# Chunks 3 to 7: VectorE adds up 768 of the 1024 columns of a V row and TensorE 256, instead of 512 each

## The chip, the core and the metric

The kernel runs on one core of one Trainium2 chip, in one launch, with all inputs in HBM. The metric is the device time of that launch in microseconds (us).

## What is computed

One decoder layer over 1024 tokens of width 1024, in float32: two groups of attention heads side by side (eight MLA heads and eight dilated-window heads), an attention over 256 memory tokens, and then PEER, a layer of single-neuron experts. The part that matters here is PEER. For each token 8 heads pick 16 experts each out of 16384, so 128 picks a token; each pick has a row of `u_tab` (dotted with the token) and a row of `v_tab` (added to the token's result with the resulting coefficient), each of 1024 float32 numbers:

```python
def peer_ffn(xn, w_q, sub_keys, u_tab, v_tab):
    def chunk(xc):                                   # 128 tokens
        ...                                          # top 16 x 16 keys -> expert (c, 8, 16), best_s
        g = jax.nn.softmax(best_s, axis=-1)
        u = u_tab[expert]
        a = jax.nn.gelu(jnp.einsum('cd,chkd->chk', xc, u), approximate=False)
        coeff = g * a
        return jnp.einsum('chk,chkd->cd', coeff, v_tab[expert])

h = h + mixed @ w_out                                # both attention groups
h = h + memory_attention(...)
h = h + peer_ffn(rms_norm(h, norm_ffn), ...)
out = rms_norm(h, norm_final)
```

## The kernel before

Tokens are worked on in 8 chunks of 128, one token a partition. After the weights have been folded (`fold_weights`) and the projections made (`project_tokens`), the attention of chunks 0 to 2 runs alone. From then on the expert rows flow in all the time. `Stream` holds their order: `ROWS` lists 2048 rows, ("u", g) or ("v", g) for pick g, U rows 22 picks ahead of V rows at first. One row is one indirect DMA that GpSimd issues (`Stream.gpsimd`, L264): for each of the 128 tokens it fetches the 4 KB of that token's expert, 512 KB in all, into one of the 8 slots of `s_ring`. A slot is free for a new row when its old row has been used: a U row by VectorE, a V row by all engines that add it up (L248 to L254).

- A U row is multiplied with the token and summed on VectorE (L380, `s_dots`). ScalarE makes Gelu of 16 dots at a time (L282), VectorE the coefficient (L368).
- A V row is multiplied with its coefficient and added to the result. TensorE does it as a matmul with a diagonal matrix of the coefficients (L454, into PSUM: `a_acc` here, `e_acc` elsewhere); the diagonal is made by ScalarE (L310, `s_diagonal`), three of them in turn. VectorE does it as a `scalar_tensor_tensor` on `s_h` in SBUF (L387).

`STAGES` says who does what. In rows 0 to 214 (picking of chunks 0 to 2) and from row 640 on (picking of chunks 3 to 7) the mode is "pe": TensorE adds up all 1024 columns. In rows 215 to 639 the mode is "split": TensorE takes columns 0 to 511 and VectorE columns 512 to 1023. These 425 rows, 212 U and 213 V, run beside the attention of chunks 3 to 7 (`attend`, first = 3), which needs six of the eight PSUM banks for itself. In this stage the token vector that U rows are multiplied with stands in SBUF (`s_x`); in the other two it is copied to PSUM (`x_copy`).

`attend` goes through 80 units, one head of one chunk each. In a unit of nb key blocks TensorE transposes the probabilities (L1297, nb of them), makes the scores of the unit after the next (L1242 or L1246) and multiplies probabilities with values (L1257); VectorE adds the bias table and takes the maximum (L1158), ScalarE does the exponential (L1108) and the copy of the transposed block (L1129). After each unit every engine works off its share of the rows, up to `rows_until[n]`, which grows with nb + 3 and in one unit of each chunk by 44 more, where the output projection of the chunk before (L1275, 32 matmuls of 512 columns) runs with rows between the matmuls. Every engine runs its instructions in the order written; no scheduler reorders them. At the end of a chunk of picks (two ends fall into the stage) VectorE adds TensorE's sum to `s_h` (L426), and at the end of the stage `flush` does (L416). A barrier ends the stage; then the last stage begins.

Of the kernel before, what the change touches and what calls it, by code (L numbers as in the profile page):

```python
# [9 lines left out]
ALU = mybir.AluOpType  # L10
# [100 lines left out]
class Stream:  # L111
# [5 lines left out]

    def __init__(self, nc, io, sb, sb_early, sem, stages):  # L120
        self.nc, self.io = nc, io
        self.stages = [(start, until, mode) for start, (until, mode) in zip([0] + [u for u, _ in stages], stages)]
        self.ident = sb("s_ident", [P, P])
        self.eps = sb("s_eps", [P, 1])
        self.h = sb("s_h", [P, D])
# [9 lines left out]
        self.more_slots = None  # L135
        self.acc = None
        self.x_copy = None

        self.row_loaded = [sem(f"s_row_loaded{i}") for i in range(WIDE_RING)]
        self.x_kept = [sem(f"s_x_kept{c}") for c in range(CHUNKS)]  # L140
# [25 lines left out]
        for n in range(len(ROWS)):  # L166
            s = next(i for i, (start, until, _) in enumerate(self.stages) if start <= n < until)
            kind = ROWS[n][0]
            pe += kind == "v"
            dve += kind == "v" and self.stages[s][2] == "split"  # L170
            self.stage_of.append(s)
            self.pe_through.append(pe)
            self.dve_through.append(dve)
            if n == wide_from:
                free = list(range(RING, WIDE_RING)) + free
            slot = free.pop(0)
            free.append(slot)
            self.slot.append(slot)
            self.before.append(last_in.get(slot))
            last_in[slot] = n  # L180
# [28 lines left out]
        return self.stages[self.stage_of[n]][2]  # L209

    def pe_columns(self, n):
        return D if self.mode(n) == "pe" else BANK

    def row(self, n):
        slot = self.slot[n]
# [24 lines left out]
    def gpsimd(self, until):  # L240
        pool = self.nc.gpsimd
        for n in range(self.at["gpsimd"], min(until, len(ROWS))):
            kind, g = ROWS[n]
            c, k = divmod(g, PICKS)
            paired = n >= PAIRS_AT
            if paired and kind == "v":
                continue
            for m in {self.before[n], self.before[n + 1] if paired else None} - {None}:  # L248
                if ROWS[m][0] == "u":
                    pool.wait_ge(self.u_used, ROWS[m][1] + 1)  # L250
                else:
                    pool.wait_ge(self.v_pe, self.pe_through[m])
                    if self.mode(m) == "split":
                        pool.wait_ge(self.v_dve, self.dve_through[m])  # L254
            if kind == "u" and k % (2 * TOPK) == 0:
                pool.wait_ge(self.expert_ready, GROUPS * c + k // (2 * TOPK) + 1)
            pool.sem_inc(self.passed_pool, 1)
            slot = self.slot[n]
            table = self.io["peer_uv" if paired else "peer_u" if kind == "u" else "peer_v"]
            to = self.row(n)  # L260
            if paired:
                to = self.ring[:, slot:slot + 2, :] if slot < RING else self.more_slots[:, slot - RING:slot - RING + 2, :]
                to = to.rearrange("p s d -> p (s d)")
            pool.indirect_dma_start(out=to, out_offset=None, in_=table,  # L264
                                    in_offset=bass.IndirectOffsetOnAxis(ap=self.expert[c % PICK_BUFFERS][:, k:k + 1], axis=0)
                                    ).then_inc(self.row_loaded[self.slot[n]], 16)
        self.at["gpsimd"] = max(until, self.at["gpsimd"])
# [63 lines left out]

    def end_root(self, c):
        act = self.nc.scalar
        act.wait_ge(self.h3_ready, c + 1)
        need(act, self.out_stored, 16 * c)
        if c + 1 < CHUNKS and LAST_U[c] >= self.stages[-1][0]:
            act.wait_ge(self.x_copied, self.copies[len(self.stages) - 1, c + 1])
        act.activation(self.scratch[:, :], self.h[:, :], ACT.Square, accum_out=self.end_stat[:, 0:1]).then_inc(self.end_squared, 1)
        act.wait_ge(self.end_squared, c + 1)
        act.activation(self.end_stat[:, 1:2], self.end_stat[:, 0:1], ACT.Sqrt, scale=1.0 / D,  # L340
                       bias=self.eps[:, :]).then_inc(self.end_rooted, 1)
        act.dma_start(self.scratch[:, :], self.io["norm_final_row"].partition_broadcast(P)).then_inc(self.final_loaded, 16)
# [9 lines left out]
    def vector(self, until):  # L352
        dve = self.nc.vector
        for n in range(self.at["vector"], until):
            kind, g = ROWS[n]
            c, k = divmod(g, PICKS)
            if n in self.end_sum_at:
                self.end_sum(self.end_sum_at[n], self.stage_of[n])
            if n in self.end_out_at:
                self.end_out(self.end_out_at[n])  # L360
            if n in COEFF_AT:
                i = COEFF_AT[n]
                d, h = divmod(i, PEER_HEADS)
                at = slice(TOPK * h, TOPK * (h + 1))
                gate = self.gate[d % PICK_BUFFERS][:, h, :]
                dve.wait_ge(self.gate_ready, GROUPS * d + h // 2 + 1)
                dve.wait_ge(self.activated, i + 1)
                dve.tensor_tensor(gate, self.active[:, at], gate, ALU.mult).then_inc(self.coeff_ready, 1)  # L368
            row = self.row(n)
            if kind == "u":  # L370
                s = self.stage_of[n]
                copied = self.mode(n) == "pe"
                if k == 0 or n in self.first_u:
                    if copied:
                        dve.wait_ge(self.x_copied, self.copies[s, c])
                    else:
                        dve.wait_ge(self.x_loaded, 16 * self.x_loads[s, c])
                self.wait_row(dve, n)
                x = self.x_copy if copied else self.x
                dve.tensor_tensor_reduce(row, row, x[:, :], 1.0, 0.0, ALU.mult, ALU.add,  # L380
                                         self.dots[:, k:k + 1]).then_inc(self.u_used, 1)
            elif self.mode(n) == "split":
                self.wait_row(dve, n)
                dve.wait_ge(self.coeff_ready, g // TOPK + 1)
                self.wait_h(c, self.dve_through[n] - 1)
                half = slice(BANK, D)
                dve.scalar_tensor_tensor(self.h[:, half], row[:, half], self.coeff(g), self.h[:, half], ALU.mult,  # L387
                                         ALU.add).then_inc(self.v_dve, 1)
        self.at["vector"] = max(until, self.at["vector"])

    def picks_free(self, c):

# [26 lines left out]
    def end_sum(self, c, s):  # L419
        dve = self.nc.vector  # L420
        last = CHUNK_END[c]
        dve.wait_ge(self.v_pe, self.pe_through[last])
        self.wait_h(c, self.dve_through[last])
        group = self.group(c, s)
        columns = slice(0, self.pe_columns(group[-1]))
        dve.tensor_tensor(self.h[:, columns], self.acc[:, columns], self.h[:, columns], ALU.add).then_inc(self.h3_ready, 1)  # L426
        dve.wait_ge(self.h3_ready, c + 1)

    def end_out(self, c):
        dve = self.nc.vector  # L430
# [7 lines left out]
    def tensor(self, until):  # L438
        pe = self.nc.tensor
        for n in range(self.at["tensor"], until):  # L440
            kind, g = ROWS[n]
            if kind == "u":
                continue
            c = g // PICKS
            s = self.stage_of[n]
            group = self.group(c, s)
            if n == group[0] and c > 0 and self.group(c - 1, s):
                pe.wait_ge(self.h3_ready, c)
            made = self.pe_through[n]
            pe.wait_ge(self.diagonal_ready, made)  # L450
            self.wait_row(pe, n)
            row = self.row(n)
            for at in range(0, self.pe_columns(n), BANK):
                last = pe.matmul(self.acc[:, at:at + BANK], self.diagonal[:, made % DIAGONALS, :], row[:, at:at + BANK],  # L454
                                 start=(n == group[0]), stop=(n == group[-1]))
            last.then_inc(self.v_pe, 1)
        self.at["tensor"] = max(until, self.at["tensor"])
# [902 lines left out]
def pick_chunks(nc, io, stream, chunks, events, until, resident):  # L1360
# [6 lines left out]
    with ExitStack() as ctx:  # L1367
# [16 lines left out]
        b.gain = stream.scratch if gain_kept else b.h  # L1384
        stream.acc = ps("e_acc", [P, D])
        stream.x_copy = ps("e_x_copy", [P, D])
        block = ctx.enter_context(nc.Block())

        def table_of(f, number):
# [376 lines left out]


PICK_02, ATTEND_37 = 215, 640
STAGES = [(PICK_02, "pe"), (ATTEND_37, "split"), (len(ROWS), "pe")]


def hybrid_layer(nc, io):
# [80 lines left out]
```

## Time and profile before

| | us |
|---|---|
| three runs | 4079.92, 4094.79, 4095.18 |
| their median | 4094.79 |
| the profiled execution, its own time | 4086.41 |
| its span, first to last instruction | 4084.6 |
| the stage with the attention of chunks 3 to 7, in that span | 1322 to 2048 |

Busy time over the whole span: TensorE (PE) 3284.0 us (80%), VectorE (DVE) 2166.0 us (53%), GpSimd (POOL) 1374.5 us (34%), ScalarE (ACT) 1300.4 us (32%). These are averages over stages with different limits, so for this change only the rows of the stage count. Busy matmuls are pipelined, and a busy PE is not a PE at its peak. In a row of a timeline the first number is the start, the second the duration; in brackets stands the idle time of the engine just before and who ended it. "issue" is a gap in which the engine waited for nothing that the profile shows.

### The profile page before, as it was taken

To read this page: it belongs to the slowest core of one execution; us is meant where nothing else is said; L and a number is where in the kernel's file an instruction comes from. 1 tells how busy PE (TensorE), PEld (TensorE's weight loads), DVE (VectorE), ACT (ScalarE), POOL (GpSimd) and SP (SyncE) were. 2 spreads that over 40 slices of the span, in tenths; PEclk is the share of its full clock that TensorE was granted. 3 is DMA by queue.
4 is the path that set the end of the run, shared out by engine and by line. 5 is a ranking of instruction groups with operands and counts; after the bars stand their busy time and mean duration, and the time that the engine had idled before them with its cause. 6 is when DMAs were issued, how large, how long until landed. Compare 5 with 4: busy or idle time off the path is not lost. (4 is left out here: it accounts for less than half of the span.)

```text
span 4084.6 us, 33485 instructions
## 1 busy us (share of the span) xinstructions
PE 3284.0 (80%) x9134; PEld 1561.4 (38%) x9134; DVE 2166.0 (53%) x4954; ACT 1300.4 (32%) x3397; POOL 1374.5 (34%) x1367
## 2 busy tenths in 40 slices
PE   8689888758784878887869689779878977987776
PEld 6544445323232444544433234234323423432222
DVE  0311112166847667766615745854774585477444
ACT  1011113211221434433323433443443344344333
POOL 0000000024533767766612233333333332333332
PEclk9889997879897899999989899999999999999999
DMA  7610112499997999998978799999999999999998
GB/s 290 226 55 23 32 51 103 141 330 384 333 326 265 363 343 368 355 376 306 361 315 300 294 372 394 420 370 379 415 383 368 405 417 359 376 416 412 422 420 354
DMA packets 283743, 1288.75 MB, mean 316 GB/s; under 512 B 27440, under 2 KB 52144, under 8 KB 193072
## 3 DMA queue, kind: packets, MB, share of 16 engines
q0 software_dynamic: 195120, 1073.83, 67.5%
q1 hardware_dynamic: 83696, 195.62, 13.1%
q10 hardware_dynamic: 4752, 17.30, 1.2%
q8 instruction: 69, 1.13, 0.1%
q14 instruction: 106, 0.87, 0.1%
HBM read 1243.65 MB, written 42.99 MB: 315 GB/s over the span
## 5 line engine op out<-in xcount | busy, mean ns | idle before, releaser
L454 PE MATMUL e_acc<-s_ring,s_diagonal 128*128 128x512 f32 x2296 | 1149.1, 629 | 353.0 <-ACT s_diagonal L310 307.4
L380 DVE CUSTOM_DVE_ANT_0 s_ring<-s_ring,e_x_copy 128x1024 f32<-128x1024 f32 x581 | 704.9, 1217 | 460.3 <-DMA s_ring<-peer_uv,s_expert 399.5
L454 PEld LDWEIGHTS e_acc<-s_ring,s_diagonal 128*128 128x128 f32 x2296 | 427.8, 197 | 1026.9 <-ACT s_diagonal L310 549.4
L264 POOL DMA_INDIRECT s_ring<-peer_uv,s_expert x462 | 435.9, 943 | 868.0 <-PE e_acc L454 687.4
L454 PE MATMUL e_acc<-e_more_slots,s_diagonal 128*128 128x512 f32 x948 | 469.8, 622 | 108.1 <-ACT s_diagonal L310 98.7
L310 ACT ACTIVATE s_diagonal<-s_ident,s_gate 128x128 f32<-128x128 f32 x1024 | 396.8, 398 | 333.3 <-PE e_acc L454 221.1
L264 POOL DMA_INDIRECT s_ring<-peer_u,s_expert x331 | 358.1, 1082 | 398.8 <-DVE s_expert L1637 232.7
L264 POOL DMA_INDIRECT s_ring<-peer_v,s_expert x325 | 347.5, 1069 | 346.9 <-PE e_acc L454 123.3
L327 ACT ACTIVATE s_dots<-s_dots 128x1 f32<-128x1 f32 x704 | 141.5, 201 | 943.2 <-DVE s_dots L380 941.9
L380 DVE CUSTOM_DVE_ANT_0 e_more_slots<-e_more_slots,e_x_copy 128x1024 f32<-128x1024 f32 x231 | 281.0, 1218 | 209.7 <-DMA e_more_slots<-peer_uv,s_expert 207.3
L264 POOL DMA_INDIRECT e_more_slots<-peer_uv,s_expert x231 | 218.4, 945 | 435.5 <-PE e_acc L454 329.1
L454 PE MATMUL a_acc<-s_ring,s_diagonal 128*128 128x512 f32 x426 | 242.9, 675 | 106.7 <-DMA s_ring<-peer_v,s_expert 53.9
L454 PEld LDWEIGHTS e_acc<-e_more_slots,s_diagonal 128*128 128x128 f32 x948 | 174.1, 195 | 382.7 <-ACT s_diagonal L310 205.8
L380 DVE CUSTOM_DVE_ANT_0 s_ring<-s_ring,s_x 128x1024 f32<-128x1024 f32 x212 | 259.5, 1224 | 111.3 <-DMA s_ring<-peer_u,s_expert 100.2
L1225 POOL TENSOR_SCALAR a_w_out<-a_w_out,a_gain_mix 128x1024 f32<-128x1024 f32 x8 | 8.8, 1109 | 616.8 <-DMA a_w_out<-w_out 616.8
L329 ACT ACTIVATE s_gate<-s_dots,s_gate 128x1 f32<-128x1 f32 x704 | 207.3, 294 | 22.9
L1129 ACT ACTIVATE a_probs_t<-a_turned 128x128 f32<-128x128 f32 (+7 forms) x128 | 83.3, 651 | 375.7 <-PE a_turned L1297 371.1
L1696 PE MATMUL e_product<-e_halves,e_rows_t 128*128 128x512 f32 x384 | 180.1, 615 | 11.7 <-ACT e_rows_t L1472 7.8
L387 DVE SCALAR_TENSOR_TENSOR s_h<-s_ring,s_gate,s_h 128x512 f32<-128x512 f32 x213 | 160.2, 752 | 48.0 <-DMA s_ring<-peer_v,s_expert 35.1
L1257 PE MATMUL a_heads_out<-values,a_probs_t 128*128 128x64 f32 x1152 | 165.4, 292 | 17.1 <-ACT a_probs_t L1129 15.0
L1257 PEld LDWEIGHTS a_heads_out<-values,a_probs_t 128*128 128x128 f32 x1152 | 152.4, 205 | 69.4 <-ACT a_probs_t L1129 50.1
L1696 PE MATMUL e_product<-e_peer_scores,e_rows_t 128*128 128x512 f32 x320 | 159.1, 592 | 0.0
(206 smaller groups left out, 3423.9 us busy)
## 6 DMA issues: line engine op xcount, KB each, us to landing
e_halves<-peer_scores SPq DMA_DIRECT2D x12, 2048.0 KB, 16.1
e_halves<-mem_scores SPq DMA_DIRECT2D x6, 2048.0 KB, 14.7
e_halves<-mem_values SPq DMA_DIRECT2D x6, 2048.0 KB, 19.7
p_w_in<-w_in SPq DMA_DIRECT2D x8, 1104.0 KB, 15.4
f_w_big<-w_mem_kv SPq DMA_DIRECT2D x4, 2048.0 KB, 15.7
f_w_big<-peer_w_q_t SPq DMA_DIRECT2D x2, 4096.0 KB, 17.8
peer_scores<-f_stage_s SPq DMA_DIRECT2D x16, 512.0 KB, 3.6
s_ring<-peer_uv,s_expert POOLq DMA_INDIRECT x462, 8.8
```

The lines of the kernel that those rows point to most:

```text
L264: pool.indirect_dma_start(out=to, out_offset=None, in_=table, in_offset=bass.IndirectOffsetOnAxis(ap=self.expert[c % PICK_BUFFERS][:, k:k ...
L310: act.activation(self.diagonal[:, made % DIAGONALS, :], self.ident[:, :], ACT.Copy, scale=self.coeff(g)).then_inc(self.diagonal_ready, 1)
L327: act.activation(self.active[:, k:k + 1], self.dots[:, k:k + 1], ACT.Gelu).then_inc(self.activated_alone, 1)
L329: act.activation(self.coeff(g), self.active[:, k:k + 1], ACT.Copy, scale=self.coeff(g)).then_inc(self.coeff_made, 1)
L380: dve.tensor_tensor_reduce(row, row, x[:, :], 1.0, 0.0, ALU.mult, ALU.add, self.dots[:, k:k + 1]).then_inc(self.u_used, 1)
L387: dve.scalar_tensor_tensor(self.h[:, half], row[:, half], self.coeff(g), self.h[:, half], ALU.mult, ALU.add).then_inc(self.v_dve, 1)
L454: last = pe.matmul(self.acc[:, at:at + BANK], self.diagonal[:, made % DIAGONALS, :], row[:, at:at + BANK], start=(n == group[0]), stop=(n ...
L1129: act.activation(probs_t[:, u % 2, 0:P * nb], turned[:, 0:P * nb], ACT.Copy).then_inc(p_t_ready, 1)
L1225: pool.tensor_scalar(w_out[:, k, :], w_out[:, k, :], gain_mix[:, k:k + 1], 1.0, ALU.mult, ALU.mult).then_inc(w_gained, 1)
L1257: last = pe.matmul(heads_out[:, HEAD * h:HEAD * (h + 1)], probs_t[:, u % 2, P * k:P * (k + 1)], keep["values"][:, k, HEAD * u:HEAD * (u + ...
L1696: made = pe.matmul(bank, b.rows_t[:, P * k:P * (k + 1)], table_of(f, number)[:, k, :], start=(k == 0), stop=(k == DT - 1))
```

## The change

`STAGES` gets a third number for each stage, the columns that TensorE takes of a V row: 1024, 256 and 1024. `pe_columns` reads it. In rows 215 to 639 the matmuls of L454 are then 128x256 instead of 128x512, the additions of L387 128x768 instead of 128x512, and the three additions of TensorE's sum to `s_h` (L426 twice, L416 once) 128x256 instead of 128x512. The number and the order of the instructions on every engine stay as they are, the waits too. The new function `add_part`, which lets VectorE take columns in a "pe" stage as well, is not called with these numbers, and `summed(c)` is c + 1.

```diff
-        self.stages = [(start, until, mode) for start, (until, mode) in zip([0] + [u for u, _ in stages], stages)]
+        self.stages = [(start, until, mode) for start, (until, mode, _) in zip([0] + [u for u, _, _ in stages], stages)]
+        self.columns = [columns for _, _, columns in stages]
...
     def pe_columns(self, n):
-        return D if self.mode(n) == "pe" else BANK
+        return self.columns[self.stage_of[n]]
+
+    def summed(self, c):
+
+        return sum(1 + (self.mode(CHUNK_END[d]) == "pe" and self.pe_columns(CHUNK_END[d]) < D) for d in range(c + 1))
...
-                half = slice(BANK, D)
-                dve.scalar_tensor_tensor(self.h[:, half], row[:, half], self.coeff(g), self.h[:, half], ALU.mult,
+                rest = slice(self.pe_columns(n), D)
+                dve.scalar_tensor_tensor(self.h[:, rest], row[:, rest], self.coeff(g), self.h[:, rest], ALU.mult,
                                          ALU.add).then_inc(self.v_dve, 1)
+            elif self.pe_columns(n) < D:
+                if n < PAIRS_AT:
+                    self.add_part(n)
...
             for at in range(0, self.pe_columns(n), BANK):
-                last = pe.matmul(self.acc[:, at:at + BANK], self.diagonal[:, made % DIAGONALS, :], row[:, at:at + BANK],
+                to = min(at + BANK, self.pe_columns(n))
+                last = pe.matmul(self.acc[:, at:to], self.diagonal[:, made % DIAGONALS, :], row[:, at:to],
                                  start=(n == group[0]), stop=(n == group[-1]))
...
-STAGES = [(PICK_02, "pe"), (ATTEND_37, "split"), (len(ROWS), "pe")]
+STAGES = [(PICK_02, "pe", D), (ATTEND_37, "split", D // 4), (len(ROWS), "pe", D)]
```

## Rows read from the trace of the kernel before

**Rows 1.** Window of the stage: length, busy time (x instructions) of PE, PEld, DVE, ACT, POOL; clock, DMA share, GB/s

```profile
1560.00:1680.00 120.00, 103.89 (x396) 58.03 (x396) 86.51 (x144) 42.58 (x88) 84.83 (x77) 0.94 0.99 374
```

**Rows 2.** Groups by form, 1320 to 2030 us: busy, mean ns; idle before

```profile
L380 DVE CUSTOM_DVE_ANT_0 s_ring<-s_ring,s_x 128x1024 f32<-128x1024 f32 x212 | 259.5, 1224 | 111.3 <-DMA s_ring<-peer_u,s_expert 100.2 <-DMA s_x<-next_x 10.6
L454 PE MATMUL a_acc<-s_ring,s_diagonal 128*128 128x512 f32 x426 | 242.9, 675 | 106.7 <-DMA s_ring<-peer_v,s_expert 53.9 <-ACT s_diagonal L310 32.1 <-issue 20.0
L264 POOL DMA_INDIRECT s_ring<-peer_u,s_expert x208 | 240.0, 1154 | 77.3 <-issue 58.6 <-DVE s_dots L380 10.8 <-DVE s_h L387 4.2
L264 POOL DMA_INDIRECT s_ring<-peer_v,s_expert x214 | 239.0, 1117 | 165.9 <-issue 49.7 <-DVE s_dots L380 46.4 <-DVE s_h L387 42.1
L387 DVE SCALAR_TENSOR_TENSOR s_h<-s_ring,s_gate,s_h 128x512 f32<-128x512 f32 x213 | 160.2, 752 | 48.0 <-DMA s_ring<-peer_v,s_expert 35.1 <-DMA s_h<-next_h 10.0
```

**Rows 3.** What GpSimd waited for, 1330 to 2020 us: total, times, longest

```profile
POOL s_ring L264 <- issue: 106.1, 337, 1.2
POOL s_ring L264 <- DVE s_h L387: 46.3, 26, 14.1
POOL s_ring L264 <- DVE s_dots L380: 36.0, 18, 5.7
POOL s_ring L264 <- PE a_acc L454: 31.5, 33, 3.3
```

**Rows 4.** Line 264 over the whole span, and the page on DMA issues: us to landing

```profile
DMA to landing us min/median/max: 4.1/7.7/46.2
...
s_ring<-peer_u,s_expert POOLq DMA_INDIRECT x331, 6.5
```

**Rows 5.** Timeline: a V row's matmuls, then the projection's

```profile
1583.65 1.02 PE L454 MATMUL a_acc<-s_ring,s_diagonal 128*128 128x512 f32 x2
1584.51 1.02 PE L1275 MATMUL a_turned<-a_w_out,a_mixed_t 128*128 128x512 f32 x2
```

**Rows 6.** Groups by form: one VectorE operation at two widths, a matmul at 256

```profile
L1158 DVE CUSTOM_DVE_ANT_0 a_probs<-a_scores,a_tables 128x768 f32<-128x768 f32 x16 | 15.2, 952 | 0.7 <-PE a_scores L1242 0.7
...
L1158 DVE CUSTOM_DVE_ANT_0 a_probs<-a_scores,a_tables 128x512 f32<-128x512 f32 x16 | 11.0, 686 | 8.4 <-PE a_scores L1242 8.4
...
L1242 PE MATMUL a_scores<-mla_k_t,a_q_mla 96*128 96x256 f32 x16 | 4.8, 379 | 0.0
```

**Rows 7.** GpSimd's groups in the stage before, 1100 to 1200 us

```profile
L264 POOL DMA_INDIRECT s_ring<-peer_u,s_expert x22 | 21.1, 960 | 6.7 <-issue 6.7
L264 POOL DMA_INDIRECT s_ring<-peer_v,s_expert x22 | 20.8, 943 | 52.1 <-PE e_acc L454 36.9 <-DVE s_dots L380 14.5 <-issue 0.6
```

**Rows 8.** Timeline: long issues on GpSimd, and VectorE beside them

```profile
1331.17 0.74 DVE L387 SCALAR_TENSOR_TENSOR s_h<-s_ring,s_gate,s_h 128x512 f32<-128x512 f32 x1
1331.44 1.29 POOL L264 DMA_INDIRECT s_ring<-peer_v,s_expert  x1 [0.30 <-issue]
...
1339.25 1.87 POOL L264 DMA_INDIRECT s_ring<-peer_u,s_expert  x1 [0.30 <-issue]
1340.34 0.75 DVE L387 SCALAR_TENSOR_TENSOR s_h<-s_ring,s_gate,s_h 128x512 f32<-128x512 f32 x1
...
2028.57 1.50 POOL L264 DMA_INDIRECT s_ring<-peer_v,s_expert  x1 [0.30 <-issue]
2029.19 0.75 DVE L387 SCALAR_TENSOR_TENSOR s_h<-s_ring,s_gate,s_h 128x512 f32<-128x512 f32 x1
```

**Rows 9.** What VectorE waited for on TensorE, 1320 to 2050 us

```profile
DVE a_mixed_t L1182 <- PE a_turned L1265: 21.5, 5, 6.7
DVE a_probs L1158 <- PE a_scores L1242: 12.3, 8, 5.5
```

**Rows 10.** Timeline: scores matmuls before and after a long wait of TensorE

```profile
1653.80 1.55 PE L1246 MATMUL a_scores<-dil_k_t,a_q_dil 64*128 64x512 f32 x4
...
1661.64 1.10 PE L454 MATMUL a_acc<-s_ring,s_diagonal 128*128 128x512 f32 x2 [2.41 <-DMA s_ring<-peer_v,s_expert]
...
1663.57 2.93 PE L1246 MATMUL a_scores<-dil_k_t,a_q_dil 64*128 64x512 f32 x4
```

More of the change, by code:

```diff
@@ L121, in __init__ @@
         self.nc, self.io = nc, io
-        self.stages = [(start, until, mode) for start, (until, mode) in zip([0] + [u for u, _ in stages], stages)]
+        self.stages = [(start, until, mode) for start, (until, mode, _) in zip([0] + [u for u, _, _ in stages], stages)]
+        self.columns = [columns for _, _, columns in stages]
+        assert all(mode == "split" or columns == D or s == len(stages) - 1 for s, (_, mode, columns) in enumerate(stages))
         self.ident = sb("s_ident", [P, P])
@@ L137, in __init__ @@
         self.x_copy = None
+        self.part = None
         self.row_loaded = [sem(f"s_row_loaded{i}") for i in range(WIDE_RING)]
@@ L169, in __init__ @@
             pe += kind == "v"
-            dve += kind == "v" and self.stages[s][2] == "split"
+            dve += kind == "v" and self.columns[s] < D
             self.stage_of.append(s)
@@ L252, in gpsimd @@
                     pool.wait_ge(self.v_pe, self.pe_through[m])
-                    if self.mode(m) == "split":
+                    if self.pe_columns(m) < D:
                         pool.wait_ge(self.v_dve, self.dve_through[m])
@@ L333, in end_root @@
         act = self.nc.scalar
-        act.wait_ge(self.h3_ready, c + 1)
+        act.wait_ge(self.h3_ready, self.summed(c))
         need(act, self.out_stored, 16 * c)
@@ L385, in vector, with add_part @@
                 self.wait_h(c, self.dve_through[n] - 1)
-                half = slice(BANK, D)
-                dve.scalar_tensor_tensor(self.h[:, half], row[:, half], self.coeff(g), self.h[:, half], ALU.mult,
+                rest = slice(self.pe_columns(n), D)
+                dve.scalar_tensor_tensor(self.h[:, rest], row[:, rest], self.coeff(g), self.h[:, rest], ALU.mult,
                                          ALU.add).then_inc(self.v_dve, 1)
-        self.at["vector"] = max(until, self.at["vector"])
+            elif self.pe_columns(n) < D:
+                if n < PAIRS_AT:
+                    self.add_part(n)
+                elif n - 2 >= PAIRS_AT:
+                    self.add_part(n - 2)
+                if n == len(ROWS) - 1:
+                    self.add_part(n)
+        self.at["vector"] = max(until, self.at["vector"])
+    def add_part(self, n):
+        dve = self.nc.vector
+        g = ROWS[n][1]
+        rest = slice(self.pe_columns(n), D)
+        row, part = self.row(n)[:, rest], self.part[:, :]
+        self.wait_row(dve, n)
+        if g >= ALONE_FROM:
+            dve.wait_ge(self.coeff_made, g - ALONE_FROM + 1)
+        else:
+            dve.wait_ge(self.coeff_ready, g // TOPK + 1)
+        if n == self.group(g // PICKS, self.stage_of[n])[0]:
+            dve.tensor_scalar(part, row, self.coeff(g), None, ALU.mult).then_inc(self.v_dve, 1)
+        else:
+            dve.wait_ge(self.v_dve, self.dve_through[n] - 1)
+            dve.scalar_tensor_tensor(part, row, self.coeff(g), part, ALU.mult, ALU.add).then_inc(self.v_dve, 1)
     def picks_free(self, c):
@@ L426, in end_sum @@
         dve.tensor_tensor(self.h[:, columns], self.acc[:, columns], self.h[:, columns], ALU.add).then_inc(self.h3_ready, 1)
-        dve.wait_ge(self.h3_ready, c + 1)
+        if self.mode(last) == "pe" and columns.stop < D:
+            rest = slice(columns.stop, D)
+            dve.tensor_tensor(self.h[:, rest], self.part[:, :], self.h[:, rest], ALU.add).then_inc(self.h3_ready, 1)
+        dve.wait_ge(self.h3_ready, self.summed(c))
     def end_out(self, c):
@@ L447, in tensor @@
             if n == group[0] and c > 0 and self.group(c - 1, s):
-                pe.wait_ge(self.h3_ready, c)
+                pe.wait_ge(self.h3_ready, self.summed(c - 1))
             made = self.pe_through[n]
@@ L1386, in pick_chunks @@
         stream.x_copy = ps("e_x_copy", [P, D])
+        if resident and stream.columns[-1] < D:
+            stream.part = sb("e_part", [P, D - stream.columns[-1]])
         block = ctx.enter_context(nc.Block())
```

## The prediction

> **What bounds the kernel now.** I looked for the stage that the change touches and asked in it which wait ends last. The stage runs from 1322 to 2048 us, 726 of the 4084.6 us, and ends in a barrier; nothing outside it changes.
>
> One window first [rows 1]. TensorE is busy 87% of it, VectorE 72%, and the 16 DMA engines 99%. GpSimd shows 84.83 us, which looks like 71%, but the gap of 0.30 us behind each issue isn't counted as busy [rows 8]: 77 x (1.10 + 0.30) = 108 of 120 us. So rows of experts come in about as fast as GpSimd can issue them and the DMA engines can carry them. TensorE's high share says nothing yet.
>
> Then the groups [rows 2]. VectorE and TensorE both wait for rows: VectorE 100.2 us for U rows and 35.1 for V rows, TensorE 53.9 for V rows. An engine that waits so much for its input isn't what sets the pace; it is fed.
>
> Last, what GpSimd waits for [rows 3]. The four lines and the busy time make up the 690 us: 470 busy in 414 issues, 106.1 of plain gaps (337 times, 0.31 each), 82.3 waiting for VectorE to free a slot (44 times, one end of a chunk with 14.1 among them) and 31.5 waiting for TensorE (33 times). In 337 of 414 cases nothing held GpSimd but its own instructions. **The stage is bound by GpSimd's issuing, with the DMA engines right behind**, and slots that are freed late cost 114 us at most. Of these TensorE has the smaller part.
>
> A cushion comes with it. A row lands 6.5 us (median) after its issue, against 4.1 at the least [rows 4]. Some 2.4 us of that is a queue in front of busy DMA engines, so an issue that comes a little later or earlier shows up only in part in when its row lands. I take one half for this below, an estimate from the DMA share of 0.99 (no idle time to recover) and the queue (which can run dry in waits over 2.4 us).
>
> **What the change takes from TensorE.** A V row costs it 0.86 us, from the start of its two matmuls to the start of the next ones [rows 5]. Half the columns should be half of that, 0.43 us; a matmul of 256 columns is there (379 ns against 675 for 512, with latency in both [rows 2, 6]), so the saving is not under 0.30 x 2 either. I take 0.43: 213 x 0.43 = 92 us of TensorE's time. It isn't on the path that sets the end except where somebody waits for TensorE. Those places are:
> - GpSimd's 33 waits for TensorE, 31.5 us [rows 3]. The gap of 0.30 stays in each, so 21.6 us can go. But a V slot is freed by both engines, and VectorE now leaves it later: it is late next. I take half, 11.
> - VectorE's 13 waits for the turned block and for scores [rows 9]. Each can shrink by what TensorE gains in a unit of two V rows, 0.86: 11 us, and half of it, 6, as the others are short.
>
> The bound is 33 us of gain; I take 17, and half of it behind the DMA queue: **-8 us**.
>
> **What it adds on VectorE.** VectorE's time grows with the width by 952 - 686 = 266 ns for 256 columns [rows 6]. L387 goes from 752 [rows 2] to 1018 ns: 213 x 0.266 = 57 us, or 8% of the stage on top of 72%. Behind L387 on VectorE stands the next U row or the next maximum (L1158), and behind these ScalarE's exponential and TensorE's transposes. Of the 135 us that VectorE waits for rows, 57 can be filled, so most of it is hidden. Where it has a backlog it isn't: GpSimd waited 44 times for a slot of VectorE, and each wait grows by 0.27 us for every V row in the backlog; one gives 12, two give 24, none gives 0. One V row lies between two frees, so I take 12, and half of it: **+6 us**.
>
> **What it does to GpSimd.** Nothing in GpSimd's code changes, and yet its instructions would. In the stage before this one an issue takes 0.95 us [rows 7], here 1.14 [rows 2]: over 422 issues 77 us more. The difference between the stages is that L380 reads both inputs from SBUF here (`s_x`), as L387 does. The timeline shows where the time goes [rows 8]. The issue at 1339.25 ends at 1341.12, and L387 beside it at 1341.09; the one at 2028.57 ends at 2030.07, L387 at 2029.94. I went through all 427 issues of the stage: 182 take over 0.98 us. Of these 72 end within 0.15 us behind an L387 (the two are the first and the last), 38 end 0.8 us behind the end of an L387 that ran when they began (the first is the one at 1331.44, ending at 1332.73, L387 at 1331.91), and 63 the same way behind an L380. So GpSimd is held until VectorE's instruction is over. L387 becomes 0.266 us longer, and the 110 issues that it holds are held so much longer: 110 x 0.266 = 29 us. If the stretch grows only with VectorE's time in such instructions, it is 57 / 420 x 77 = 10 us. Between the two I take 20, nearer to the count, since I saw the ends coincide, but less, since some issues will fall elsewhere. GpSimd sets the pace, so half of it gets through: **+10 us**.
>
> The Trainium skill, SBUF — State Buffer, "Who interferes with whom", says that a VectorE instruction with two SBUF inputs contends with a GpSimd one that reads SBUF, but infers that descriptor generation isn't held by it, because it needs the write side. The trace contradicts that inference [rows 7, 8]. By the inference this term would be 0 and the sum 10 us lower, still no change.
>
> **The rest.** The three additions of TensorE's sum lose 0.27 us each, and TensorE's last two V rows before the final projection 0.4 us each: **-1 us**. ScalarE's work stays as it is.
>
> **Sum.** -8 + 6 + 10 - 1 = +7 us. The profiled execution took 4086.4 us, 1.8 more than its span, and would take 4093. It lies 8 us under the median of the three runs and 4 under their mean, 4090.0, which I build on because the three spread over 15 us: **4097 us**.
>
> **Rivals.**
> - *TensorE is the bound after all.* For: it is busy 87%, more than any other compute engine. If all that was waited for it comes back and VectorE's longer additions vanish in its waits for rows: -33 us, 4057 us, faster. Against: TensorE itself waits 53.9 us for rows, and the DMA engines have hardly a gap. Chance 0.17.
> - *VectorE holds GpSimd.* Slower by one mechanism: every one of the 110 held issues is held 0.266 us longer, and the DMA queue doesn't cushion it since the delay comes again and again: +29, with the 12 of late slots whole, less 8: +33 us, 4123 us. It decides as soon as more than about two thirds of the 29 us reach the stage's end. For: the ends that coincide [rows 8], and 337 issues with nothing else in front [rows 3]. Against: the queue of 2.4 us. Chance 0.31.
> - *TensorE's clock.* Less work on it means more pauses, and behind a pause of 2.41 us four matmuls took 2.93 us instead of 1.55 [rows 10], the lower of the two clocks, 1.2 instead of 2.4 GHz. If the granted clock fell from 0.94 to 0.85, 18% more of 726 us would run at half speed and cost TensorE about 65 us of work. That is less than the 92 it is given, so the time would be that of the forecast. I count it there.
>
> **How the numbers follow.** A measurement of this kernel can tell about 0.5% (20 us) from no change. Forecast (within 0.5%) 0.52, slower 0.31, faster 0.17. The bounds of the terms together reach from -34 (33 + 1, nothing lost) to +53 (29 + 24, nothing won), 4056 to 4143; cut to eight in ten this is 4062 to 4135. The likeliest case alone has 4070 to 4110.
>
> **What would show it.** In the profile after: L387 at about 1018 ns; L454 of `a_acc` with half the start-to-start time; GpSimd's mean issue in the stage up from 1.14 to about 1.18 us, with ends that still coincide with L387's (at 1.14 or less that term is wrong); GpSimd's waits for TensorE under 20 us and for VectorE over 82; VectorE's waits for rows down from 135 us; the barrier at 2048 moved by less than 20 us. If the barrier comes 30 us earlier and GpSimd's waits shrink on both engines, the pace was TensorE's, and my reading of rows 3 was wrong. If it comes 30 us later with issues at 1.2 us or more, the halving was wrong.

## The result and the profile after

The changed kernel takes 4101.09 us (median of 20 runs, 4089.95 to 4108.11), the kernel before 4087.07 us (20 runs, 4079.53 to 4096.43). The ratio is 1.0033, with a 95% interval of 1.0024 to 1.0042: 14 us slower, within the 0.5% that were called no change. Timed again beside other kernels (e10 below) it was 1.0038 (1.0024 to 1.0052).

The profiled execution of the changed kernel has a span of 4097.8 us. Its stage with the attention of chunks 3 to 7 ends with the barrier at 2064.7 us, where it ended at 2047.7 before. That is 17 us later, 1 of which was already there when the stage began. So the loss is in the stage. (A span is that of one execution; the runs of one kernel spread over 17 to 18 us here, so a few microseconds between two profiles mean nothing by themselves.) The stage of both kernels as one window each, before first (columns as in rows 1):

```profile
1322.00:2048.00 726.00, 601.44 (x2350) 338.68 (x2350) 506.51 (x860) 269.03 (x535) 481.84 (x425) 0.93 0.94 352
```
```profile
1323.00:2065.00 742.00, 577.11 (x2350) 388.25 (x2349) 559.42 (x860) 269.71 (x535) 509.30 (x425) 0.82 0.93 344
```

Three numbers moved. VectorE is 53 us busier, as it should be. GpSimd is 27.5 us busier, although nothing in its code was changed. And TensorE is only 24 us less busy, with its granted clock down from 0.93 to 0.82. The 27.5 us are of one profile each: in a second profile of the changed kernel (e10) GpSimd's 425 issues take 497.2 us, 15 us more than before, at the same loss of time. So GpSimd's growth lies between 15 and 28 us. These are the groups by form of the changed kernel that answer to [rows 2]:

```profile
L388 DVE CUSTOM_DVE_ANT_0 s_ring<-s_ring,s_x 128x1024 f32<-128x1024 f32 x212 | 259.2, 1223 | 77.3 <-DMA s_ring<-peer_u,s_expert 65.6 <-DMA s_x<-next_x 11.1
L490 PE MATMUL a_acc<-s_ring,s_diagonal 128*128 128x256 f32 x426 | 161.9, 490 | 143.3 <-DMA s_ring<-peer_v,s_expert 84.4 <-ACT s_diagonal L318 37.0 <-issue 21.5
L272 POOL DMA_INDIRECT s_ring<-peer_u,s_expert x208 | 245.3, 1179 | 76.4 <-issue 46.0 <-DVE s_h L395 12.9 <-DVE s_dots L388 10.7
L272 POOL DMA_INDIRECT s_ring<-peer_v,s_expert x214 | 261.2, 1221 | 153.3 <-PE a_acc L490 52.2 <-issue 47.9 <-DVE s_h L395 44.3
L395 DVE SCALAR_TENSOR_TENSOR s_h<-s_ring,s_gate,s_h 128x768 f32<-128x768 f32 x213 | 217.0, 1019 | 56.1 <-DMA s_ring<-peer_v,s_expert 44.0 <-DMA s_h<-next_h 9.9
```

L395 takes 1019 ns, as worked out. TensorE waits more for V rows (84.4 us instead of 53.9): it comes to them earlier, or they come later; the rows shown don't tell which. VectorE waits less for rows (110 us instead of 135): it has less time to spare. The matmuls of V rows lost 81 us of busy time, but TensorE as a whole only 24, so its other matmuls in the stage grew by 57 us. The largest of their groups, before first and then after (busy us, mean ns); the transposes of L1297 went from 293 to 332 ns:

```profile
L1257 PE MATMUL a_heads_out<-values,a_probs_t 128*128 128x64 f32 x960 | 125.9, 283 | 11.4 <-ACT a_probs_t L1129 9.9 <-DVE a_mixed L1169 1.5
```
```profile
L1293 PE MATMUL a_heads_out<-values,a_probs_t 128*128 128x64 f32 x960 | 143.1, 307 | 11.5 <-ACT a_probs_t L1165 9.9 <-DVE a_mixed L1205 1.6
```

What GpSimd waited for in the changed kernel, 1330 to 2035 us, against [rows 3]:

```profile
POOL s_ring L272 <- issue: 92.1, 302, 0.3
POOL s_ring L272 <- PE a_acc L490: 59.0, 49, 19.6
POOL s_ring L272 <- DVE s_h L395: 56.9, 56, 15.0
POOL s_ring L272 <- DVE s_dots L388: 19.5, 8, 4.7
```

The 19.6 us are the start of the stage, a wait that lay just outside the window before and was put down to VectorE there. Without it GpSimd waits 39.4 us for TensorE (31.5 before) and 76.4 for VectorE (82.3 before). The account of GpSimd's time is then +27.5 busy, -14 in plain gaps, +8 and -6: the stage's 16 us. The term that stands out is GpSimd's own busy time. Where it comes from shows in the timeline. This is one of 71 such pairs of the changed kernel:

```profile
1587.37 1.02 DVE L395 SCALAR_TENSOR_TENSOR s_h<-s_ring,s_gate,s_h 128x768 f32<-128x768 f32 x1
1587.65 1.54 POOL L272 DMA_INDIRECT s_ring<-peer_v,s_expert  x1 [0.30 <-issue]
```

The issue begins at 1587.65 while L395 runs, L395 ends at 1588.39, and the issue ends 0.80 us later, at 1589.19, where an undisturbed one takes 0.94 us in all. Below, an issue is called held when it takes over 0.98 us and ends 0.8 us behind a VectorE instruction that ran when it began; the hold is what it takes over 0.94 us.

### The profile page after: what moved, and what is told of

Read it like the earlier page. It is cut to its first block and busy times, and to the rows that moved or that the text cites. A ratio compares the mean times of both kernels' runs of the same rounds, so it can differ in the third digit from the quotient of the medians.

```text
span 4097.8 us, 33485 instructions
## 1 busy us (share of the span) xinstructions
PE 3257.8 (80%) x9134; PEld 1612.5 (39%) x9134; DVE 2219.0 (54%) x4954; ACT 1301.5 (32%) x3397; POOL 1403.2 (34%) x1367
## 3 DMA queue, kind: packets, MB, share of 16 engines
q8 instruction: 69, 1.13, 0.1%
## 5 line engine op out<-in xcount | busy, mean ns | idle before, releaser
L388 DVE CUSTOM_DVE_ANT_0 s_ring<-s_ring,e_x_copy 128x1024 f32<-128x1024 f32 x581 | 704.9, 1217 | 465.2 <-DMA s_ring<-peer_uv,s_expert 403.0
L272 POOL DMA_INDIRECT s_ring<-peer_v,s_expert x325 | 369.7, 1137 | 332.4 <-PE e_acc L490 123.2
L388 DVE CUSTOM_DVE_ANT_0 e_more_slots<-e_more_slots,e_x_copy 128x1024 f32<-128x1024 f32 x231 | 281.0, 1218 | 210.4 <-DMA e_more_slots<-peer_uv,s_expert 208.0
L388 DVE CUSTOM_DVE_ANT_0 s_ring<-s_ring,s_x 128x1024 f32<-128x1024 f32 x212 | 259.2, 1223 | 77.3 <-DMA s_ring<-peer_u,s_expert 65.6
L490 PE MATMUL a_acc<-s_ring,s_diagonal 128*128 128x256 f32 x426 | 161.9, 490 | 143.3 <-DMA s_ring<-peer_v,s_expert 84.4
L395 DVE SCALAR_TENSOR_TENSOR s_h<-s_ring,s_gate,s_h 128x768 f32<-128x768 f32 x213 | 217.0, 1019 | 56.1 <-DMA s_ring<-peer_v,s_expert 44.0
L1293 PEld LDWEIGHTS a_heads_out<-values,a_probs_t 128*128 128x128 f32 x1152 | 171.9, 227 | 73.3 <-ACT a_probs_t L1165 47.2
L1293 PE MATMUL a_heads_out<-values,a_probs_t 128*128 128x64 f32 x1152 | 184.4, 315 | 15.8 <-ACT a_probs_t L1165 13.7
L490 PEld LDWEIGHTS a_acc<-s_ring,s_diagonal 128*128 128x128 f32 x426 | 85.1, 231 | 208.5 <-issue 146.9
## 6 DMA issues: line engine op xcount, KB each, us to landing
e_halves<-mem_values SPq DMA_DIRECT2D x6, 2048.0 KB, 19.6
```

The source lines that it names most:

```text
L395: dve.scalar_tensor_tensor(self.h[:, rest], row[:, rest], self.coeff(g), self.h[:, rest], ALU.mult, ALU.add).then_inc(self.v_dve, 1)
L490: last = pe.matmul(self.acc[:, at:to], self.diagonal[:, made % DIAGONALS, :], row[:, at:to], start=(n == group[0]), stop=(n == group[-1]))
L1293: last = pe.matmul(heads_out[:, HEAD * h:HEAD * (h + 1)], probs_t[:, u % 2, P * k:P * (k + 1)], keep["values"][:, k, HEAD * u:HEAD * (u + ...
```

## Experiments

The two theories: **A**, the change costs time because VectorE's longer instruction with two SBUF inputs holds GpSimd's issues longer; in a second form, because VectorE's longer time makes everything behind it later, whoever is held. **B**, the loss is TensorE's, which is slower with the lower clock. The runs came in three sessions (e1 to e4; e7 to e10; e5, e6, e11 and e12), and their times for the kernel before differ (medians 4109, 4099 and 4090 us). So each ratio is against runs of the kernel before from the same session, and spans of different sessions aren't compared. The changed kernel was timed with the result and in the second session, not in the first and the third, so a comparison of e3, e4 or e12 with it is one of two ratios. 12 us are 0.3%.

### e1 and e2: each half of the change alone

```diff
-                half = slice(BANK, D)
+                half = slice(BANK // 2, D)
```

> VectorE's half of the change alone: L387 of the kernel before takes columns 256 to 1023 (768 wide), TensorE keeps its 512, so columns 256 to 511 are added twice. Theory A (GpSimd's issues are held by VectorE's longer two-input instructions, 479 us of issues becoming 506 in the changed kernel): GpSimd's issues take about 506 us here too, TensorE's clock in the stage stays near 0.93, and the time is that of the changed kernel or more, +14 to +20 us over the kernel before. Theory B (the loss is TensorE's, whose granted clock in the stage fell from 0.93 to 0.82 and which made all its other matmuls there 57 us longer): with TensorE's work back the clock is back, and the time is within 5 us of the kernel before.

Measured: 1.0024 (1.0004 to 1.0043), +10 us; window 1322 to 2066:

```profile
1322.00:2066.00 744.00, 597.27 (x2327) 335.39 (x2328) 560.00 (x862) 269.67 (x537) 495.69 (x423) 0.92 0.93 343
```

```diff
-        return D if self.mode(n) == "pe" else BANK
+        return D if self.mode(n) == "pe" else BANK // 2
```

> TensorE's half of the change alone: the matmuls of a V row in the split stage are 256 wide, VectorE keeps its 512, so columns 256 to 511 are not added at all. Theory A (VectorE holds GpSimd): issues stay near 479 us, and TensorE's relief is worth 0 to -8 us. Theory B (TensorE's clock): the clock in the stage falls to 0.85 or less though VectorE does nothing more, GpSimd waits for TensorE as long as before or longer, and the time is +5 to +15 us.

Measured: 1.0003 (0.9989 to 1.0016), no difference.

```profile
1322.00:2066.00 744.00, 570.24 (x2353) 383.89 (x2351) 507.94 (x864) 270.78 (x540) 474.93 (x429) 0.83 0.94 348
```

VectorE's half costs time with the clock at 0.92. TensorE's half costs nothing, though it alone brings the clock to 0.83. Theory B doesn't explain a loss of 14 us: e2's interval ends at +7. But e2 says something else too: TensorE's relief brought nothing. The V rows' matmuls lost 83 us of busy time (159.7 us left of 242.9), TensorE as a whole 31 (601 to 570), the rest went to slower matmuls elsewhere, and GpSimd waited longer for TensorE than before, not less. e1's GpSimd takes 1.17 us an issue (495.69 us for 423) against 1.13 before; that is what e10, the changed kernel again, shows too, though not the 506 us that were expected. The interval allows anything from +2 to +18 us; its lower end is just clear of none.

### e3 and e4: the same time on VectorE with one SBUF input

```diff
-                dve.scalar_tensor_tensor(self.h[:, rest], row[:, rest], self.coeff(g), self.h[:, rest], ALU.mult,
-                                         ALU.add).then_inc(self.v_dve, 1)
+                dve.tensor_reduce(self.h[:, D - 1:D], row[:, D - 836:D], AX_X, ALU.max).then_inc(self.v_dve, 1)
```

> The changed kernel with L395 replaced by a reduction of 836 columns of the row, of about the same duration (1.02 us) but with one SBUF input instead of two; V rows are thus not added up on VectorE. Theory A: what held GpSimd behind a V row's addition is gone, its issues in the stage fall from 506 us by the 30 us that stand behind L395 to about 476, and the time falls by 10 to 20 us, to about the kernel before or under it. Theory B: nothing changes for TensorE, so the time stays within 5 us of the changed kernel.

Measured: 1.0007 (0.9988 to 1.0026). The reduction takes as long as the addition did, 1021 ns against 1019, and all waits are still there:

```profile
L395 DVE TENSOR_REDUCE s_h<-s_ring 128x1 f32<-128x836 f32 x213 | 217.5, 1021 | 53.3 <-DMA s_ring<-peer_v,s_expert 37.2 <-DMA s_h<-next_h 9.5 <-issue 4.1
...
L272 POOL DMA_INDIRECT s_ring<-peer_v,s_expert x217 | 243.9, 1124 | 193.3 <-PE a_acc L489 83.6 <-issue 50.9 <-DVE s_h L395 46.8
L272 POOL DMA_INDIRECT s_ring<-peer_u,s_expert x208 | 231.5, 1113 | 83.7 <-issue 49.3 <-DVE s_h L395 16.4 <-DVE s_dots L388 13.4
```

GpSimd is busy for 475 us (243.9 + 231.5), 34 less than in the changed kernel, and of the 14 us 3 are left (the interval reaches from -5 to +11). VectorE's time and TensorE's work are the same as in the changed kernel, and the clock is even lower (0.80), so neither can be what the loss came from. Against e10's profile GpSimd is busy 22 us less, not 34.

The edit takes away two things, the second input and the 768 columns of output (the reduction writes one). Which of them holds GpSimd, the trace of the kernel before tells. Outside the stage L380 writes the same 1024 columns to SBUF and takes as long, but its second input stands in PSUM:

```profile
L380 DVE CUSTOM_DVE_ANT_0 s_ring<-s_ring,e_x_copy 128x1024 f32<-128x1024 f32 x581 | 704.9, 1217 | 460.3 <-DMA s_ring<-peer_uv,s_expert 399.5 <-DMA s_ring<-peer_u,s_expert 60.6
```

410 issues of GpSimd begin while it runs so, and none takes over 0.945 us. Inside the stage, with `s_x` in SBUF, 142 of 158 are held. So it is the second input from SBUF, not the output.

e4 does the same to U rows as well (`dve.tensor_reduce(self.dots[:, k:k + 1], row, AX_X, ALU.add)` in place of L388).

> As the run before, and the products of U rows in the split stage (L388) also replaced by a reduction of all 1024 columns (same 1.22 us, one SBUF input), so the dots are wrong. Theory A: no issue of GpSimd is held any more, 0.94 to 0.96 us each, about 400 us in the stage instead of 506; if GpSimd's issuing sets the pace, the time falls by 40 to 70 us under the changed kernel; if the DMA engines stand right behind it, only by 15 to 30. Theory B: within 5 us of the changed kernel.

Measured: 0.9995 (0.9978 to 1.0011). Now nothing holds GpSimd, and each issue takes 0.937 us:

```profile
L272 POOL DMA_INDIRECT s_ring<-peer_v,s_expert x217 | 203.2, 936 | 267.0 <-PE a_acc L492 118.8 <-DVE s_h L398 56.4 <-issue 44.7
L272 POOL DMA_INDIRECT s_ring<-peer_u,s_expert x208 | 194.8, 937 | 78.9 <-issue 61.0 <-DVE s_h L398 7.7 <-DVE s_dots L392 6.8
```

398 us instead of 509, but the time is only that of the kernel before, some 16 to 18 us under the changed one. That is the branch of theory A in which something else stands right behind GpSimd's issuing. What GpSimd saved it spends waiting for slots, most of it for TensorE (118.8 us in front of V rows). With e3 it says that the hold costs time only in part of its range.

### e10, e7, e8 and e9: what the kernel before is bound by

> The changed kernel itself, beside the three runs below on the same chip. It was 14 us over the kernel before; VectorE's half alone was 10 us over it and TensorE's half alone within 2. Both theories expect +10 to +16 us.

Measured: 1.0038 (1.0024 to 1.0052).

e7 is the kernel before with the edits of e4, 580 columns for a V row (754 ns, where the addition took 752).

> The kernel before, with both of VectorE's instructions on rows of the split stage replaced by reductions of about the same duration with one SBUF input (1024 columns for a U row, 580 for a V row, 0.75 us); dots and the V half on VectorE are thus wrong. The same at VectorE's 768 columns and TensorE's 256 was at the time of the kernel before. Theory A1 (the change costs time only by holding GpSimd): without the holding the widths don't matter, and this is also at the kernel before, within 5 us. Theory A2 (the longer time on VectorE itself costs, since slots come free later and the next maximum starts later; the holding costs besides): this is 10 to 20 us under the kernel before.

Measured: 0.9998 (0.9985 to 1.0011). GpSimd is busy for 398 us as in e4. With nobody holding GpSimd, VectorE's width (e4 against e7) makes no difference: -0.05% and -0.02% against the kernel before. This is theory A in its first form. In its second form VectorE's longer time would cost by itself, and e7 would lie 10 to 20 us lower. (The two were timed in different sessions, and each interval is some 6 us wide on either side.)

e8 is e7 with half the bytes:

```diff
+            if self.mode(n) == "split":
+                to, table = to[:, 0:BANK], table.rearrange("n (two d) -> (n two) d", two=2)
```

> As the run before, and in the split stage each indirect DMA fetches 2 KB for a token instead of 4 (from the table seen as 32768 rows of 512), so that half of each slot keeps old numbers; GpSimd's issues, TensorE and VectorE do the same work. If the DMA engines bound the stage: its DMA share falls from 0.93 to about 0.5 and the time by 60 us or more. If GpSimd's issuing or the waits among the compute engines bound it: the time falls by less than 25 us.

Measured: 0.9967 (0.9948 to 0.9986), -13 us.

```profile
1322.00:2066.00 744.00, 608.13 (x2349) 350.88 (x2348) 494.12 (x648) 270.64 (x541) 406.84 (x429) 0.89 0.68 209
```

Halving the bytes of the rows and freeing GpSimd at once gives 13 us of a stage of 726. The DMA share falls only to 0.68, not to 0.5. So neither the DMA engines nor GpSimd set the pace alone; some 13 us under them (6 to 21) something else does. Which chain that is wasn't tested; the attention's own over TensorE, ScalarE and VectorE is the likely one, and TensorE is busy 82% of the window.

> The kernel before with L387 on 256 columns instead of 512 (columns 512 to 767 are not added at all), 0.49 us instead of 0.75; TensorE as before. The widening from 512 to 768 cost 10 us. Theory A (VectorE's time counts): the same step the other way, -5 to -12 us. If VectorE's width counts only above a threshold: within 3 us of the kernel before.

Measured: 1.0009 (0.9992 to 1.0025), no difference, and no gain of 5 to 12 us: a miss for theory A as it was put there. GpSimd is busy for 466 us. Neither here nor in e7 does less holding than in the kernel before (482 us) bring anything.

### e12 and e11: whose second input it is, and with TensorE's clock kept

e12 is the changed kernel with only the U rows' products as a reduction.

> The changed kernel, with the U rows' products of the split stage (L388) replaced by a reduction with one SBUF input (same 1.22 us; the dots are wrong), and the V rows' additions left as they are, 768 columns with two SBUF inputs. In the traces so far most of what GpSimd is held stands behind U rows (141 issues against 66). Theory A1 (the total that GpSimd is held decides, whichever instruction does it): its issues fall from about 500 us to 430 or less, and the time to within 5 us of the kernel before. Theory C (something about the V rows' additions themselves costs, such as their own two reads): the time stays at +10 to +16 us.

Measured: 0.9970 (0.9953 to 0.9988), 12 us under the kernel before, some 27 under the changed one.

```profile
L272 POOL DMA_INDIRECT s_ring<-peer_v,s_expert x217 | 223.4, 1030 | 193.5 <-PE a_acc L493 56.5 <-DVE s_h L398 49.3 <-issue 45.5
L272 POOL DMA_INDIRECT s_ring<-peer_u,s_expert x208 | 219.8, 1056 | 82.2 <-issue 49.9 <-DVE s_dots L392 15.1 <-PE a_acc L493 9.0
...
L398 DVE SCALAR_TENSOR_TENSOR s_h<-s_ring,s_gate,s_h 128x768 f32<-128x768 f32 x213 | 216.4, 1016 | 50.5 <-DMA s_ring<-peer_v,s_expert 37.4 <-DMA s_h<-next_h 10.0
```

The wide addition with two inputs is still there (1016 ns), and the loss is gone all the same, as GpSimd's total fell (443 us). That speaks against the addition itself as the cause. But the run is better than theory A expected, and better than e4, e7 and e9, which say that less holding than before brings nothing. That isn't explained. e4 and e12 were timed in different sessions, and their intervals (0.9978 to 1.0011, 0.9953 to 0.9988) overlap a little.

> TensorE's 512 columns as in the kernel before, and for V rows on VectorE a reduction of 836 columns with one SBUF input (1.02 us, as long as 768 columns are with two; the V half is wrong). VectorE's half alone with two inputs was +10 us. Theory A1: within 5 us of the kernel before, since GpSimd isn't held more. Theory A2 (VectorE's longer time costs by itself): +10 us as with two inputs. TensorE's clock in the stage is expected at 0.90 or more, against 0.80 where TensorE had 256 columns.

Measured: 1.0013 (0.9996 to 1.0031), +5 us, at the edge of A1. An issue takes 1.13 us, as in the kernel before. Against e1 (1.0024) it leans the way of theory A, but the intervals overlap, so it decides nothing. The clock is 0.93, as expected.

### e5 and e6: half of the change, and once and a half

The third number in `STAGES` becomes 384 and 128.

> Half of the change: TensorE 384 columns, VectorE 640. If the loss grows evenly with the width, +5 to +9 us; if it sets in at a threshold between 512 and 768, either under 3 us or the full +14.

Measured: 1.0011 (0.9994 to 1.0029), +4 us, between the two answers expected; the interval (-2 to +12) shuts out only the full 14.

> The change and half of it again: TensorE 128 columns, VectorE 896 (1.15 us). Theory A1: GpSimd's issues rise above 515 us and the time to +20 to +35 us, more than in proportion, as nothing covers the holding any more. If the loss has come to its end with 768: +10 to +16 us.

Measured: 1.0064 (1.0039 to 1.0088), +26 us (16 to 36). Its window:

```profile
1322.00:2066.00 744.00, 586.07 (x2338) 410.83 (x2338) 584.28 (x859) 269.65 (x535) 505.00 (x425) 0.72 0.93 342
```

| VectorE's columns | ratio | GpSimd, us an issue | TensorE's clock |
|---|---|---|---|
| 512 | 1 | 1.13 | 0.92 |
| 640 (e5) | 1.0011 | 1.14 | 0.86 |
| 768 (the change, e10) | 1.0033, 1.0038 | 1.20, 1.17 | 0.82, 0.82 |
| 896 (e6) | 1.0064 | 1.19 | 0.72 |

The loss grows with the width: 4, 14 and 26 us. A straight line fits the intervals as well as a curve or a threshold. GpSimd's busy time doesn't grow in step: at 896 it is 505 us and not over 515, as was expected, and the loss is larger all the same. There the clock is at 0.72, and VectorE is busy 79% of the window.

The sum of all holds in the window from 1322 to 2066 us, counted in each profile, beside the time:

| run | held, us | time against before, us |
|---|---|---|
| e4, e7 | 0, 0 | -2, -1 |
| e8, with half the bytes | 0 | -13 |
| e12 | 44 | -12 |
| e9, e2, e3 | 66, 72, 76 | +4, +1, +3 |
| e11, the kernel before, e5 | 82, 83, 85 | +5, 0, +4 |
| e1 | 98 | +10 |
| the change, e10 | 110, 97 | +14, +16 |
| e6 | 105 | +26 |

Up to the 83 us of the kernel before, the hold has no effect on the time that these runs can tell, e12 and e8 apart. The runs with more of it are those with a loss. It explains the step to 768 columns (e3, e4), but not the size of the one to 896, where the hold is no longer than in the changed kernel.

## Why the prediction was right, and where it wasn't

The forecast was no change and 4097 us; 4101 us were measured, a loss of 14 us where 7 were worked out. Step by step:

**The costs of the instructions were right.** L395 takes 1019 ns (1018 worked out), and TensorE's saving on V rows was 81 us by busy time (92 worked out by start-to-start times).

**The term for GpSimd held the loss, and was sized too small for the time and counted in a wrong way.** Its issues were to grow by 20 us; they grew by 27.5 in one profile and by 15 in the other (1.20 and 1.17 us an issue, where 1.18 was the sign asked for). That half of it gets through was an estimate, and no single share fits: above the hold of the kernel before the loss is about as large as the growth in one profile (16 of 15, e10) and half of it in the other (14 of 27.5), and below it next to nothing gets through (e4, e7). e3, where the hold behind V rows is gone, gives 11 of 14 us back. But the count behind the bound of 29 was misread. The 72 issues that end within 0.15 us behind an L387 aren't held by it. L387 begins as L380 ends and takes 0.75 us, and a held issue ends 0.8 us behind what held it, so both ends coincide by the lengths of the instructions. The pair of [rows 8] at 1339.25, with the row that the prediction left out:

```profile
1339.08 1.23 DVE L380 CUSTOM_DVE_ANT_0 s_ring<-s_ring,s_x 128x1024 f32<-128x1024 f32 x1 [0.95 <-DMA s_ring<-peer_u,s_expert]
```

L380 ends at 1340.31, the issue at 1341.12, 0.81 later. L387, from 1340.34 to 1341.09, runs beside just this part of the issue and doesn't lengthen it. Counted by that rule all but one of the 182 long issues of the kernel before fall into place: 142 are held by L380 (72 us over 0.94 each) and 39 by L387 (11 us). In the changed kernel it is 146 (79 us) and 71 (32 us). (In e10 it is 138 and 62, 71 and 26 us.) So the growth isn't 110 issues held 0.27 us longer. It is 23 to 32 more issues that meet a V row's addition, and longer holds for those that do.

**The gain on TensorE's side was wrong in sign.** GpSimd's waits for TensorE were to fall below 20 us; they rose from 31.5 to 39.4 (41.0 in e10). The rival on the clock had said what was missing: a granted clock of 0.85, 65 us of TensorE's work lost. It was 0.82 and 57 us. It had concluded that the time would be that of the forecast, and e2, no difference, agrees. But the -8 us of the sum assumed the relief without the clock, and those two can't both stand. In e2 the relief alone gave nothing.

**The waits for VectorE's slots** were to rise by 12 us (6 of them on the time) and fell by 6 (4 in e10). That GpSimd, issuing more slowly, asks for the slots later would explain it, but wasn't tested. So the sum had a gain of 8 that wasn't there, a cost of 6 that didn't show, and too small a term for GpSimd: errors of opposite sign, and +7 came near to +14 in part for that reason. Luck had a part in the 4097 us too: the kernel before was taken at 4090.0 from three runs, and twenty gave 4087.07, which hid 3 of the 7 us.

**"The stage is bound by GpSimd's issuing, with the DMA engines right behind" was too strong.** In e7 GpSimd has 84 us less to do and the time is the same; in e8 the bytes are halved too, and it is 13 us less. GpSimd's waits for slots grow instead, in e7 from 114 to some 200 us. A plain gap in front of 337 of 414 issues shows that nothing was ahead of GpSimd at that moment, not that the stage would be shorter if it were faster. In the kernel before several limits lie close together (13 of the stage's 726 us in e8). What the change took from TensorE brought nothing (e2), and what it gave VectorE reached GpSimd and cost time (e1, e3). That it had to lose isn't shown: e12 has the same columns and is 12 us faster than the kernel before.

The rule of the Trainium skill (SBUF — State Buffer, "Who interferes with whom") that a VectorE instruction with two SBUF inputs contends with a GpSimd one that reads SBUF is borne out: 1.12 to 1.22 us an issue with such instructions on VectorE, 0.94 with reductions of the same length in their place (e4, e7). The prediction took the trace to contradict the page's inference that descriptor generation isn't held by them. It doesn't go so far. What is held is only the first 0.14 us of an issue; the other 0.8 us run at their usual length even where another two-input instruction runs beside them, as L387 does above. That is so in 142 of the held issues of the kernel before. In 115 more such an instruction begins inside an issue that found none running, and 114 of these take 0.95 us at most. So a read at the start of the issue, held, and the rest of it, not held, would fit both the rule and the inference. What GpSimd does in these 0.14 us no trace here shows. The term of the sum stands all the same, as an issue is held once.

What stays open: why e12 is 12 us faster than the kernel before and e4 isn't, what makes up the loss at 896 columns, and by which path a longer hold reaches the end of the stage, since the profiles show only that both grow.

## What to carry to other kernels

When work is shared between two engines, look at what its form on the new engine does to a third one: here the longer addition of a V row filled waits of VectorE, but held GpSimd's DMA issues. A busy share of 87% on an engine that waits for input in the same stage is no reason to relieve it; here the relief came back as a lower clock and longer waits. And a hold is worked out from when an instruction begins and what runs at that moment; ends that coincide can come from the lengths of the instructions alone. Before a gain is booked for the engine with the most plain gaps, ask who would be late if it were faster: here removing 84 us of its work moved nothing.

## What the runs showed of the hardware

- An indirect DMA's issue on GpSimd takes 0.94 us undisturbed. If a VectorE instruction with two SBUF inputs runs when it begins, it ends about 0.8 us after that instruction's end. This fits 181 of the 182 long issues before and 217 of 219 after. Not held are issues that find less than about 0.14 us of the instruction left, and those that begin within 0.1 us after it: 17 of the 199 that began with over 0.17 us of it left before, 20 of 239 after. A two-input instruction that begins later in the issue doesn't hold it.
- It is the second input from SBUF that holds. A reduction of the same length with one SBUF input holds none (no issue over 0.98 us among 425 in e4). The product of a U row that writes as much to SBUF but has its vector in PSUM holds none either (410 issues begun beside it, 0.945 us at most). Of the three long issues in the window of [rows 7] two stand beside a `tensor_tensor` with two SBUF inputs (L1628, L1570) and one beside a `tensor_scalar` (L1545), so other instructions can hold an issue too.
- TensorE's granted clock in the stage follows the columns of a V row that it adds up: 0.92 at 512, 0.86 at 384, 0.82 at 256 and 0.72 at 128. In e2, where VectorE has no more to do, it is 0.83 at 256. With more of the stage at 1.2 instead of 2.4 GHz TensorE's other matmuls take longer, in the changed kernel 57 us of the 81 that its V rows gave up.
